# Eighteen dense units of a two-layer block taken by quarters, with seven products each

## The reference, cut to what matters

```
# first layer, after the scan, the attention and the gates
y_s = (y_s * silu(z_s)) @ w_ssm_out          # units so0, so1
y_a = (y_a * silu(z_a)) @ w_attn_out         # unit ao (512 rows, 1024 columns)
x   = x + (sigmoid(r_s)*y_s + sigmoid(r_a)*y_a) @ w_o         # wo0, wo1
# second layer
proj = rms_norm(x) @ w_in      # hf, hq as before; hi, hog, dq, dk, dv, gate_hg (2 units), gate_da (2 units)
o_hg = rms_norm(hgrn2(hq, hf, hi)) * silu(hog);  y_hg = o_hg @ w_branch_hg             # bhg
qn, kn = rope(rms_norm(dq)), rope(rms_norm(dk));  y_da = rms_norm(diff_attention(qn, kn, dv)) @ w_branch_da   # bda
x = x + (sigmoid(gate_hg)*y_hg + sigmoid(gate_da)*y_da) @ w_out                          # wout0, wout1
x = x + mixture_of_experts(rms_norm(x))      # 32 experts, 201 MB of weights
```

## Time and profile before

| | before |
|---|---|
| median of three runs | 1157.85 us |
| profiled execution, its own time | 1155.91 us |
| its span, first to last instruction | 1154.0 us |
| PE busy | 978.7 us (85%) |
| DVE busy | 447.0 us (39%) |
| ACT busy | 252.0 us (22%) |
| POOL busy | 164.8 us (14%) |
| mean granted clock of PE | 0.941 of full |

### The profile page before, as it was taken

How to read it: one execution, slowest core, us unless ns; L and a number is a source line. 1 busy time by engine, 2 the same in 40 slices (tenths; PEclk the granted TensorE clock), 3 DMA queues, 4 the chain that set the end, 5 groups by cost and what they waited for, 6 DMA issues and landing times. The chain is left out here.

```text
span 1154.0 us, 11360 instructions
## 1 busy us (share of the span) xinstructions
PE 978.7 (85%) x4440; PEld 478.6 (41%) x4440; DVE 447.0 (39%) x743; ACT 252.0 (22%) x613; POOL 164.8 (14%) x123
## 2 busy tenths in 40 slices
PE   8999999999989999999899999867585757575755
PEld 7644444446878446644444446312121212121211
DVE  6869999986622123353622413201010101010201
ACT  4464757333421012232122011000000000000000
POOL 1856666661000010000000000000000000000000
PEclk9999999999999999999999998988888988888788
DMA  9333242334224433443132695999999999999996
GB/s 365 154 145 146 74 146 80 139 146 121 74 93 164 166 105 135 154 156 144 57 146 92 272 400 199 430 426 428 430 427 428 427 428 428 430 428 429 428 428 282
DMA packets 22316, 292.84 MB, mean 254 GB/s; under 512 B 2752, under 2 KB 2816, under 8 KB 4480
## 3 DMA queue, kind: packets, MB, share of 16 engines
q1 hardware_dynamic: 21728, 291.69, 62.2%
q0 software_dynamic: 544, 0.56, 0.6%
HBM read 291.18 MB, written 1.05 MB: 253 GB/s over the span
## 5 line engine op out<-in xcount | busy, mean ns | idle before, releaser
L1967 PE MATMUL psum<-mem 128*32 128x512 f32 x1016 | 145.7, 706 | 84.1 <-DMA mem<-in_experts 84.0
L305 PE MATMUL psum<-mem,hT 128*128 128x512 f32 x416 | 183.9, 598 | 1.6 <-ACT xres L645 1.6
L312 PE MATMUL psum<-mem,hT 128*128 128x512 f32 x288 | 126.7, 596 | 2.8 <-ACT xn L645 1.6
L305 PE MATMUL psum<-mem 128*128 128x512 f32 x288 | 125.2, 593 | 2.4 <-ACT mem L1381 1.5
L305 PEld LDWEIGHTS psum<-mem,hT 128*128 128x128 f32 x416 | 78.4, 192 | 95.9 <-issue 95.8
L1986 PE MATMUL psum<-mem 128*32 128x512 f32 x512 | 79.6, 753 | 35.7 <-DMA mem<-in_experts 31.6
L1967 PEld LDWEIGHTS psum<-mem 128*32 128x32 f32 x1016 | 31.1, 119 | 180.3 <-DMA mem<-in_experts 118.5
L312 PEld LDWEIGHTS psum<-mem,hT 128*128 128x128 f32 x288 | 55.7, 196 | 68.3 <-issue 68.3
L305 PEld LDWEIGHTS psum<-mem 128*128 128x128 f32 x288 | 54.2, 190 | 69.0 <-issue 65.1
L319 PE MATMUL psum<-hT,mem 128*128 128x256 f32 x256 | 57.6, 382 | 0.0
L2088 DVE TENSOR_TENSOR mem<-mem,psum 128x512 f32<-128x512 f32 x8 | 5.5, 688 | 129.6 <-PE psum L1967 129.6
(11 more groups left out here) (372 smaller groups left out, 1194.0 us busy)
## 6 DMA issues: line engine op xcount, KB each, us to landing
mem<-in_experts SPq DMA_DIRECT2D x95, 2048.0 KB, 35.5
mem<-in_front SPq DMA_DIRECT2D x39, 2048.0 KB, 7.7
mem<-in_front SPq DMA_DIRECT2D x2, 1024.0 KB, 9.9
xn<-in_xT SPq DMA_DIRECT2D x1, 1024.0 KB, 6.3
mem<-in_ssm_b SPq DMA_DIRECT2D x2, 512.0 KB, 11.9
mem<-in_ssm_c SPq DMA_DIRECT2D x2, 512.0 KB, 17.8
xres<-in_x SPq DMA_DIRECT2D x1, 1024.0 KB, 9.6
mem<-in_experts SPq DMA_DIRECT2D x1, 1024.0 KB, 22.2
```

The source lines that it names most:

```text
L305: ins = pe.matmul(dst, lhs[:, k, P * i:P * i + P], w[:, k, c0:c0 + 512], start=(k == 0), stop=(k == nk - 1))
L312: ins = pe.matmul(dst, tokens[:, k, i], w[:, k, :], start=(k == 0), stop=(k == KD - 1))
L1967: ins = pe.matmul(banks[m // 4][32 * q:32 * q + 32, :], xgT[:, k, 32 * q:32 * q + 32], w[q][:, FF * kk:FF * kk + FF], start=(k == 0), stop ...
```

## The change

Each of the eighteen units named in `QUARTERED` is cut into four quarters of weights, and the tokens by features into four quarters. The unit is then computed from seven products of quarters (the Strassen and Winograd form) in the place of eight. A product is 4 matmuls of 256 columns (2 of 512 for ao, bhg, bda), so a unit has 28 matmuls of 256 or 14 of 512. POOL makes four sums of weight quarters for each unit (128x1024 each, from 18 units 72 instructions); DVE makes four sums of token quarters for each of seven inputs; ACT copies products 1 and 5 out of PSUM; DVE puts the others together with SBUF results. Each unit has three banks in turn. In dq, dk, hi, dv, hog the fills that ACT copied are now put together by DVE, and the norm with rotation is cut in passes that stand between them. The output norm of the recurrence is cut in two (`norm_sums`, `norm_out`). In an attention piece the gate unit runs 4 products, then 3. Expert units for ring slots 3 and 4 are loaded later. All else stays.

```diff
+        QUARTERED = ("so0", "so1", "ao", "wo0", "wo1", "dq", "dk", "hi", "dv", "hog", "ghg0", "ghg1", "gda0", "gda1", "bhg", "bda", "wout0", "wout1")
+        ORDERS = {name: (4, 1, 5, 6, 2, 3, 7) if name in ("wo0", "wout0") else (1, 5, 6, 2, 3, 7, 4) for name in QUARTERED}
...
+        def sums_of(dve, X, x):
+            x11, x12, x21, x22 = halves_of(X)
+            s1, s2, s3, s4 = x_sums[x]
+            link(dve, dve.tensor_tensor(s1, x21, x22, ALU.add), sums_ready)
+            link(dve, dve.tensor_tensor(s2, s1, x11, ALU.subtract), sums_ready)
+            mark(dve.tensor_tensor(s4, x12, s2, ALU.subtract), sums_ready)
+            link(dve, dve.tensor_tensor(s3, x11, x21, ALU.subtract), sums_ready)
...
+        def sum_weights(pool, n):
...
+            pool.wait_ge(slot_loaded[order[name] % SLOTS_BLOCKS], 16 * (order[name] // SLOTS_BLOCKS + 1))
+            if j >= 2:
+                pool.wait_ge(product_full, full(n - 2, 4))
+            pool.tensor_tensor(t1, w12, w11, ALU.subtract).then_inc(weights_ready, 1)
+            pool.wait_ge(weights_ready, sums_done(n, 1))
+            if j >= 1:
+                pool.wait_ge(product_full, full(n - 1, 6))
+            pool.tensor_tensor(t2, w22, t1, ALU.subtract).then_inc(weights_ready, 1)
+            pool.wait_ge(weights_ready, sums_done(n, 2))
+            if j >= 1:
+                pool.wait_ge(product_full, full(n - 1, 5))
+            pool.tensor_tensor(t4, w21, t2, ALU.subtract).then_inc(weights_ready, 1)
+            pool.tensor_tensor(t3, w22, w12, ALU.subtract).then_inc(weights_ready, 1)
...
+        def products(pe, n, X, x, which):
...
+                elif turn.index(p) >= 3:
+                    after_taken(pe, n, turn[turn.index(p) - 3])
...
+        def use_11(dve, n, use, then=None):
+            p1 = taken_of(n)[0]
+            put_11(dve, n, p1)
+            dve.wait_ge(taken, used(n, P2))
+            link(dve, use(0, 0, p1), q_step)
+            if then:
+                then(0, 0)
...
+        def use_quarters(dve, n, use, then=None):
+            take_p6(dve, n)
+            use_11(dve, n, use, then)
+            use_12(dve, n, use, then)
+            take_p7(dve, n)
+            use_22(dve, n, use, then)
+            use_21(dve, n, use, then)
+
+        def add_to_x(dve, n, c):
...
+            take_p6(dve, n)
+            with_p1 = mark(onto(x(0, 0), p1), q_step)
+            dve.wait_ge(p5_copied, n + 1)
+            mark(onto(x(0, 1), p5), q_step)
+            with_p5 = mark(onto(x(1, 1), p5), q_step)
+            dve.wait_ge(product_full, full(n, 2))
...
-            project_all(["so0", "so1"], PJ_SO, gs)
+            for j in range(2, 4):
+                pj.after_read(pe, PJ_ZA + j)
+            ORDER, TURNED = ORDERS["so0"], ORDERS["wo0"]
+            for n in range(2):
+                products(pe, n, gs, X_GS, ORDER)
...
+            products(pe, nth["ao"], oaT, X_OA, ORDER)
+            turn_quarters(pe, TP_M, m_tok, m_done)
...
-            sp.wait_ge(m_done, 4)
-            load_ahead(sp, 3)
...
+                    sp.wait_ge(m2_done, 4)
+                    load_ahead(sp, 4)
                     load_first(sp, 1)
+            load_ahead(sp, 3)
             sp.wait_ge(logits_full, 1)
...
+            pool.wait_ge(m_done, 4)
+            for n in range(OF_FIRST, len(QUARTERED)):
+                sum_weights(pool, n)
...
+            act.wait_ge(taken, used(nth["hog"], P4))
+            act.activation(og_, oda_, ACT.Tanh, scale=0.5).then_inc(th_hog, 1)
...
+            take_p6(dve, nth["dq"])
+            put_upper("dq")
+            put_rest("dq")
+            put_last("dq")
+            head_sums(0)
+            take_p6(dve, nth["dk"])
+            head_scale(0)
+            put_upper("dk")
+            put_rest("dk")
+            rope2(0, 0)
+            put_last("dk")
+            rope2(0, 1)
...
```

More of the change, by code:

```diff
@@ L427, in build @@
                         + [(f"glu{n}", PJ_GLU + 4 * n + 3) for n in range(2)]
-                        + [(f"so{n}", PJ_SO + 2 * n + 1) for n in range(2)]
-                        + [("za", PJ_ZA + 3)]
-                        + [("ao", PJ_AO + 3)] + [(f"wo{n}", PJ_WO + 2 * n + 1) for n in range(2)]):
+                        + [("za", PJ_ZA + 3)]):
             last_fill[name] = s
+        QUARTERED = ("so0", "so1", "ao", "wo0", "wo1", "dq", "dk", "hi", "dv", "hog", "ghg0", "ghg1", "gda0", "gda1", "bhg", "bda",
+                     "wout0", "wout1")
@@ new lines, in build, with full, sums_done, used @@
+        x_sums[X_M2] = x_sums[X_H2]
+        x_sums = {x: [ap.rearrange("p (k t) -> p k t", t=P) for ap in parts] for x, parts in x_sums.items()}
+        def full(n, p):
+            return 7 * n + ORDERS[QUARTERED[n]].index(p) + 1
+        def sums_done(n, t):
+            return 4 * n + (1, 2, 4, 3)[t - 1]
+        P6, P2, P3, P7, C22, P4 = range(1, 7)
+        def used(n, which):
+            return 6 * n + which
+        def after_taken(pe, n, p):
+            if p == 1:
+                pe.wait_ge(p1_copied, n + 1)
+            elif p == 5:
+                pe.wait_ge(p5_copied, n + 1)
+            else:
+                pe.wait_ge(taken, used(n, {6: P6, 2: P2, 3: P3, 7: P7, 4: P4}[p]))
@@ new lines, in build, with product_bank @@
+        FIRST_BANK = {"so0": 0, "so1": 7, "ao": 0, "wo0": 14, "wo1": 20, "dq": 0, "dk": 7, "hi": 14, "dv": 21, "hog": 28, "ghg0": 0, "ghg1": 7, "gda0": 14, "gda1": 21,
+                      "bhg": 0, "bda": 7, "wout0": 0, "wout1": 0}
+        def product_bank(n, p):
+            name = QUARTERED[n]
+            width = 2048 // blocks_of(n)
+            if ORDERS[name][0] == p == 4:
+                return banks[0][:, 0:width]
+            at = ORDERS[name].index(p) - (1 if ORDERS[name][0] == 4 else 0)
+            three = (0, 1, 6) if name in GATES else (4, 5, 6) if name in ("ao", "bhg", "bda", *INPUTS2) else (6, 7, 5) if name == "wout1" else (1, 2, 3)
+            return banks[three[(FIRST_BANK[name] + at) % 3]][:, 0:width]
@@ new lines, in taken_of @@
+        def taken_of(n):
+            name, width = QUARTERED[n], 2048 // blocks_of(n)
+            part = lambda ap: [whole[:, 0:width] for whole in four(ap)]
+            if n < OF_FIRST:
+                return part(area[:, 16896:18944]) + [area[:, 13824:14336] if name == "ao" else area[:, 18688:18944]]
+            if name in INPUTS2:
+                return part(work[:, 6144:7168]) + [None]
+            if name in GATES:
+                return part(xn[:, 1, :]) + [None]
+            return part(work[:, 2048:4096] if n < nth["wout0"] else area[:, 12288:13312]) + [xn[:, 1, 0:512]]
@@ L1179, in vector_of_first_layer @@
             dve.wait_ge(xre_in, 16)
[L1180 to L1184, removed]
+            for c in range(2):
+                add_to_x(dve, nth[f"wo{c}"], c)
             dve.wait_ge(lbe_ready, 1)
@@ L1228, in da_turned @@
             return TP_DA + (a + 2 if a else 0)
[L1229 to L1234, removed]
+        last_fill["hf"], last_fill["hq"] = PJ_HF + 3, PJ_HQ + 3
         (e1_, e2_, e3_, e4_, hq_, hv_, ket_, o_, f_, k_, b_, d_, st_, state_, og_, hgT_, oda_, daT_) = carve(
@@ L1355, in _ @@
             act.activation(b_, f_, ACT.Ln).then_inc(ln_ready, 1)
[L1357 to L1362, removed]
+            copy_p1(act, nth["dq"])
+            copy_p5(act, nth["dq"])
             act.wait_ge(diff_ready, 1)
@@ L1581, in _ @@
+            products(pe, nth["bhg"], hgT, X_HG, ORDER[1:2])
+            pe.wait_ge(taken, used(nth["gda1"], P4))
+            products(pe, nth["bhg"], hgT, X_HG, ORDER[2:6])
             pe.wait_ge(oda_ready, 1)
             turn(TP_DO, 2, by_k(oda))
+            da.after_read(pe, 7)
+            products(pe, nth["bhg"], hgT, X_HG, ORDER[6:])
             for s in range(2):
                 tp.after_read(pe, TP_DO + s)
-            w = unit_ready(pe, "bda")
-            for n in range(4):
-                s = PJ_BDA + n
-                pj.to_fill(pe, s)
-                pj.filled(project(pe, w, n % 2, pj.tile(s)[:, :], daT, c0=512 * (n // 2)), s)
@@ L1590, in _ @@
-            pe.wait_ge(m2_done, 4)
-            turn(TP_M2, 4, by_k(m2))
-            for s in range(2):
-                tp.after_read(pe, TP_M2 + 2 + s)
+            products(pe, nth["bda"], daT, X_DA, ORDER)
+            turn_quarters(pe, TP_M2, m2, m2_done)
+            for s in range(TP_M2, TP_M2 + 2):
+                tp.after_read(pe, s)
+            n0, n1 = nth["wout0"], nth["wout1"]
+            products(pe, n0, m2T, X_M2, TURNED[0:1])
+            for s in range(TP_M2 + 2, TP_M2 + 4):
+                tp.after_read(pe, s)
@@ new lines, in _ @@
+            dve.wait_ge(gates_ready, 2)
+            use_11(dve, n, of_hg)
+            use_12(dve, n, of_hg)
+            take_p7(dve, n)
+            use_22(dve, n, of_hg)
+            for s in range(2):
+                tp.after_read(dve, TP_DO + s)
+            sums_of(dve, daT, X_DA)
+            use_21(dve, n, of_hg)
+            dve.wait_ge(gates_ready, 4)
```

(3 more changed lines are left out.)

606 lines of the change are left out of this document (410 added, 196 removed).

## The result

The changed kernel takes 1211.6 us (median of 4 runs, 1208.0 to 1213.3) against 1157.1 us for the kernel before on the same chip (4 runs): 1.0448 times as long, 95% interval 1.0417 to 1.0479. Forecast were 1172 us and a range of 1140 to 1186. The direction was right; the loss is 54.5 us by the medians, 52.1 in the profiled executions, where 14 were forecast. The profiled execution took 1207.98 us (span 1206.2, against 1154.0). One execution of the kernel before that took 4679 us, in the second set of experiments, is left out of the ratios.

The account below looks back on a forecast made before the run. PE bounds up to the router, expert transfers after, so PE's start on the experts sets the end. Waits less products +12.8, clock +1.4: +14.2 on 1155.91 gives 1170.1; the median is 1.9 higher, so 1172 us (1140 to 1186).

Parts of the forecast that it names:

- What bounds: Expert transfers bound the end, PE the part before; the end moves one for one with PE's start on the experts.
- Products, -28.6: All eighteen units: seven products for eight save 1.56 us in fifteen units and 1.72 in three, -28.6 us in all.
- The rule of DVE behind POOL's running instruction: While POOL works, DVE gets one instruction with two SBUF operands through per POOL instruction, 2.2 us each.
- The loads were hidden: Weight loads stay hidden; late loads for slots 3 and 4 are covered before PE needs them, uncovered 2 us.
- POOL's sum at 2.15: Each 128x1024 weight subtraction on POOL takes 2.15 us, between trace rows of 1.95 (one repeated column) and 2.36.
- The lists: Orders of the five instruction lists, followed with fixed durations to find PE's waits; total +6.8 at 1.95, +24 at 2.36.
- Terms 1 to 6, idle time: Six stretches, first layer to router: new PE waits less those gone and saved product time, sum +12.8 us.
- turns after ao and bda: PE waits 4.7, 2.3 and 0.9 us around the transposes there, in place of 1.51, 0.73 and 0.3.
- dq to hog: DVE gets added quarter work and waits beside POOL's sums: 13.9 us new PE waits, products -7.8, net +6.1.
- the 10.7 of the term: Attention pieces: 10.7 us of new PE waits against products and stalls gone, net -1.7 us.
- Term 7, the clock: PE's matmuls slow down behind waits above 3 us; one more dip counted, +1.4 us, range 0 to +7.
- contention in full and the clock: Rival, 1182 to 1190 us, chance 0.14: POOL's sums take 2.36, long PE waits lower the clock, +24 + 5.

Follow-up runs that it names:

- the second set of experiments: Second of three sets of follow-up runs: four kernels run beside the kernel before, whose median there was 1159.6 us.
- the last version: Changed kernel with POOL's sums in four instructions each and added matmuls in PE's remaining waits, none in dq, dk, dv, hog: 1150.8 us.
- halves: Changed kernel with each of POOL's sums made in two instructions of 128x512, the same elements in all: 1181.9 us.
- fourths: Changed kernel with each of POOL's sums made in four instructions of 128x256, the same elements in all: 1157.5 us.

## Why the prediction was right in its mechanism and wrong in its size

- **What bounds.** Right: PE started on the experts 53.4 us later and the span grew by 52.2; the expert stage kept its length but for 1.1 us.
- **Products, -28.6.** Right: 288.8 us of own matmuls in the last version against 317.0 - 28.6 = 288.4.
- **The rule of DVE behind POOL's running instruction.** Right, for instructions with two SBUF operands: 7.32 us for three additions, and the fall with halves and fourths. The loads were hidden and POOL was never waited for.
- **POOL's sum at 2.15.** Wrong: 2.36, the upper end and the value of the one row with two full operands. The row that was nearest in form should have been taken, not a mean with the other. The lists had 11.2 us of waits for it; measured 8.0, and 12 to 14 with the slow matmuls that go with them. By the table in the Trainium skill ("GPSIMD Engine Reference", section 3.1), which is of an addition and not of a subtraction as the prediction has it, the estimate was 2.25, nearer than what was taken, and still short of the 2.36 of the trace.
- **Terms 1 to 6, idle time.** Forecast +41.4 us net at 2.15, which is +52.6 at 2.36; measured +49.0. By place: turns after ao and bda 4.7 + 2.3 + 0.9 each, measured 5.43 + 1.67 and 0.8 for ACT; between wo0 and wo1 2.3, measured 3.04 and 3.05; dq to hog 13.9, measured 6.54 + 2.19 + 0.66 + 4.23 + 4.20 = 17.8; ahead of the recurrence's output 3.0, measured 3.1. Followed from six durations, this part held. That one-operand scalings and copies wait as well was not in the rule. The copy of 2.87 us stands in dq to hog, which came out 3.9 us above its term. The four scalings of 2.40 us stand in the attention pieces, and there the waits are 2.88 + 0.34 + 2.27 + 2.28 + 2.90 = 10.7 us, the 10.7 of the term all the same: something else in it was too high by as much, and what was not looked into, so that agreement is luck.
- **Term 7, the clock, +1.4 in a range of 0 to 7.** This is the step that failed: it measured +31.7. It was sized from one wait and the half unit behind it, 1.4 us, times one. Two things were wrong. The count: instead of one net dip the trace has twelve intervals at the lower level (1.2 GHz), 82 us of the stretch in all, where before had one of 3.4 us; the means of the two windows, 0.89 and 0.99, say the same. 12 of the 14 waits of 2.19 us or more have slow matmuls behind them (3.78 us for 1.89, 5.38 for 3.62, 6.55 for 3.62). And the length: the recurrence, whose matmuls are small, had a mean clock of 0.67 over 21.3 us and lost 5.4 there behind a wait of 3.13. The rival "contention in full and the clock" named both causes, and its sign came true (the wait in `add_to_x` was 3.04 and 3.05 us, over its 2.9). But it had 5 us for the clock and 0.14 as its chance, and its 1182 to 1190 stops short of the measured 1211.6 as well: no case of the prediction reached it.

With 2.36 in the lists and the measured clock the sum is -28.6 + 52.6 + 31.7 = +55.7, 3.6 over the +52.1 measured. The expected gain was thus lost twice: to DVE waiting for POOL, and to PE's clock behind the waits that this made.

## What to carry to other kernels

Before work is given to an idle POOL, follow the DVE chains that stand ahead of a PE wait and charge each SBUF-only instruction in them, copies and scalings too, one whole POOL instruction (here 2.4 us; reductions went free); if the work must go there, cut POOL's instructions short, even if POOL gets slower in sum, as long as PE does not come to wait for POOL. A wait of PE costs itself and the slow matmuls behind it: here 49 us of waits brought 32 us more, so an unpriced clock term can turn a sum. Where waits stay, matmuls in a spare bank can win the second part back, but only where the granted clock is below 1.00.

## What the runs showed that was not expected

- The slow part costs two thirds to four fifths of the waits that cause it: 31.7 us on 49.0 in the change, 9.9 on 12.2 in the kernel before with POOL's sums beside it.
- The clock does not fall at once: behind the 3.13 us wait three groups of matmuls ran at 0.44 and 0.43, then the same ones took 0.69.
- Cutting 128x1024 sums into fourths costs POOL a third more time (231 us for 173) and saves the kernel 54 us.
- With one source for both operands POOL's 128x1024 subtraction took 1.97 us on average, DVE's instructions between them included, against 2.36 and more for two sources. Why was not tested; it also means that the idle sums hold DVE for less time each than the change's.
